# A decoder step on one core: half of the quarter-stack requests of tiles 3 to 6 asked for by ScalarE

## The chip, the cores and the metric

The kernel runs on one core of a Trainium2 chip. Its time is the device time of one execution in microseconds. The profile is of one execution, taken by the hardware profiler. PE is TensorE's matmul stream, DVE is VectorE, ACT is ScalarE, POOL is GpSimd, SP is SyncE. "SPq" and "ACTq" mark requests for transfers (DMAs) that an engine issues; the transfers themselves run on the core's 16 DMA engines.

## The reference

One layer of a decoder over 1024 prompt tokens and 32 sample tokens, in float32. A combined projection feeds latent attention and a chunked retention; both are gated, mixed, added to the input and normalised (`h`). Then comes the part around the change: a shared expert, and for each token 6 of 64 routed experts, summed with weights, and a last normalisation:

```
eidx, ew = route(h2d, w_router, router_bias)              # 6 experts and weights for a token
ffn = routed_experts(h2d, eidx, ew, ...) + swiglu(h2d, w_sh_gate, w_sh_up, w_sh_down)
y   = layer_norm(DEEPNORM_ALPHA * h + ffn, ln2_g, ln2_b)
```

`routed_experts` multiplies each token's row by the gate, up and down matrices of its six experts and adds the six results, each times its weight.

## The kernel before, in words

Tokens lie in nine tiles of 128 rows (`NT = 9`, `P = 128`, `D = 1024`); tile 8 holds only the 32 sample tokens. The kernel runs in stages one after the other: projection, retention, attention, mixing, trunk (normalisation and routing), experts. The change is at the end of `experts`.

In the expert stage a loop goes over blocks of up to 128 gathered token rows, one expert each. TensorE multiplies, and GpSimd scatters each block's results to the table `y_rows` in HBM (`put_rows`, L2470). That table has 8 rows of 4 KB for each token, of which rows 0 to 5 are its six experts' results. Each scatter increments `y_out[c]`.

The last stage adds the six rows of each token with their weights, adds the shared expert's result and alpha times `h`, and normalises. For tiles 0 to 7 the work is split:

- rows 4 and 5 of each token come as a "pair" (1 MB a tile, `pair`, L2379) and are added to `acc[t]` by VectorE (`add_row`, L2656), two additions a tile in the order of the tiles; each increments `added`.
- rows 0 to 3 come as a "stack" of 2 MB a tile (`stack`, L2386): four quarters q of 512 KB, each with the 32 tokens 32q to 32q+31 of the tile, 128 rows of 4 KB. Each quarter is one transfer and adds 16 to `stack_in[b]`. TensorE sums them with 16 small matmuls against a weight matrix (`routed`, L2890) after `stack_in[b]` has reached 64 times the use of that buffer.
- the shared expert's down product of a tile is eight matmuls (`shared_down`, L2863) into the same accumulator before `routed`. TensorE issues it two tiles ahead: after those of tiles 0, 1, 3 and 2 the order is routed 0, routed 1, routed 2, shared 4, routed 3, shared 5, and so on. There are four accumulators `S` (e_G, e_T, e_Y, e_A); the shared product of tile i waits until tile i-4 is joined.
- the sample tokens (tile 8) have their own small rows (`small`, L2390), a small shared product (L2867) and a small routed product (L2876).

VectorE then works tile by tile: `join` (L2716, alpha times `acc` plus the accumulator, with the row sum), `mean`, `scaled` of the tile before (L2755), `variance`, `gain` (L2745). ScalarE computes the sums of squares (`squares`, L2563), GpSimd the reciprocal root (L2493). SyncE writes each finished tile out (L2447).

Seven stack buffers serve eight tiles (`stack_of`). Tiles 0, 1 and 2 use buffers that expert weights held; tiles 3, 4, 5 and 6 use memory in which the pairs of tiles 0 to 7 lay, so their requests wait until those pairs are added; tile 7 uses the buffer of tile 0 again and waits for `pe_done`, which `routed` increments.

All of these requests are issued by SyncE, in this order: after the last rows are written (`rows_written(NE)`, a wait for both `y_out`) the stacks of tiles 0, 1, 2; then for tiles 3 to 6 a wait `pair_added(2 * t - 5)`, which is `added >= 4, 8, 12, 16`, and the stack; then a wait for `pe_done` and the stack of tile 7; then the six small rows; then the outputs as they become ready. ScalarE issues none in this stage. An engine carries its instructions out in order, and SyncE and ScalarE have a hardware queue each in front of the same 16 DMA engines (queue 1 and queue 10 in the profile).

Of the kernel before, what the change touches and what calls it, by code (L numbers as in the profile page):

```python
# [28 lines left out]
P = 128  # L29
D = 1024  # L30
KD = D // P
NT = 9
# [17 lines left out]
NE, TOPK, FF = 64, 6, 256  # L50
# [10 lines left out]
NS = DB * DQ  # L61
# [2191 lines left out]
def experts(nc, passed, begun, parts, acc_in, acc, pair_in, pairs, stack_in, stacks, w_stack, sel, small_rows, junk, shared, ident, wb, gu_in, ready, w_d, d_in, ln2, ln2_rows, ln2_in, a, h_rows, tok_list, meta, y_rows, out_p, out_s):  # L2253

    with ExitStack() as ctx:
        sb = lambda n, s, d=F32: ctx.enter_context(nc.sbuf_tensor("e_" + n, s, d))
        sem = lambda n: ctx.enter_context(nc.semaphore("e_" + n))
        W = 4
# [14 lines left out]
        stacks = stacks + [nc.alloc_sbuf_tensor_at("stack6", [P, 4, D], F32, offset=w_hi_at)]  # L2273
# [14 lines left out]
        small_w_ok, small_ok, pl, diag_ok, part_ok, pe_done, added, joined, shift_ok, sq_ok, var_ok, rstd_ok, gained, out_ok, o_out = [  # L2288
            sem(n) for n in "small_w_ok small_ok pl diag_ok part_ok pe_done added joined shift_ok sq_ok var_ok rstd_ok gained out_ok o_out".split()]
        stack_of = [(5, 1), (3, 1), (6, 1), (0, 1), (4, 1), (1, 1), (2, 1), (5, 2)]  # L2290
# [5 lines left out]
        y_out = [sem(f"y_out{c}") for c in range(2)]  # L2296
# [6 lines left out]
        def wait_alone(eng, s, value):  # L2303
            eng.wait_ge(s, value)
            eng.sem_inc(passed, 1)

        def quads(eng):

            return eng.value_load(meta[P:P + 1, 0:1], min_val=1, max_val=OVER // W)
# [4 lines left out]
        def at(eng, r, mul, add):  # L2314

            return r * mul + add if isinstance(r, int) else eng.snap(r * mul + add)
# [7 lines left out]
        def _(sp):  # L2324
# [8 lines left out]
            more = quads(sp)  # L2333
# [45 lines left out]
                sp.dma_start(pairs[t][:].rearrange("p k n -> p (k n)"),  # L2379
                             y_rows.rearrange("(t k) n -> t (k n)", k=8)[t * P:(t + 1) * P, 4 * D:6 * D]).then_inc(pair_in[t], 16)  # L2380

            def stack(t):

                b = stack_of[t][0]
                for q in range(4):
                    sp.dma_start(stacks[b][:, q, :], y_rows.rearrange("(t k) n -> t k n", k=8)[t * P + NS * q:t * P + NS * (q + 1), 0:4, :]).then_inc(stack_in[b], 16)  # L2386

            def small(k):
# [16 lines left out]
            def pair_added(t):  # L2405

                sp.wait_ge(added, 2 * t + 2)
# [27 lines left out]
            for t in range(3):  # L2435
                stack(t)
            for t in range(3, NT - 2):
                pair_added(2 * t - 5)
                stack(t)
            sp.wait_ge(pe_done, 1)  # L2440
            stack(NT - 2)
            for k in range(TOPK):
                small(k)
# [51 lines left out]
        @block.scalar  # L2495
        def _(act):
            s_ = nc.scalar

            def gate(n, c):
                act.wait_ge(gu_done, n)  # L2500
                s_.activation(sig[:, c, :], G[c][:, 0:FF], ACT.Sigmoid).then_inc(sig_ok, 1)

            def turned_act(n, c):
                act.wait_ge(a_turned, n)
                s_.copy(aT[:, c].rearrange("p k n -> p (k n)"), A[:, 0:2 * P]).then_inc(aT_ok, 1)

            def turned(n, c):
                act.wait_ge(x_turned, n)
                s_.copy(xT_hi[:, c].rearrange("p k n -> p (k n)"), GX[1][:].rearrange("p q n -> p (q n)")).then_inc(xT_act, 1)  # L2509

            def rounded(s, n_in, c, part):
                act.wait_ge(gu_in[s], n_in)
                for j in (2 * part, 2 * part + 1):
                    s_.copy(w_hi[c][:, :, 2 * j:2 * j + 2, :], w_gu[s][:, :, 2 * j:2 * j + 2, :]).then_inc(w_hi_ok, 1)  # L2514

            def kept(n, c, stored):
                act.wait_ge(d_done, n)
                if stored is not None:
                    wait_alone(act, y_out[c], stored)
                s_.copy(y_sb[:, c, 0:512], Y[0][:]).then_inc(y_act, 1)  # L2520

            gate(1, 0)
            for s in range(1, W):
                turned(2 * s + 4, 1 - s % 2)
                for part in range(2):
                    if s >= 2:
                        if part == 0:
                            kept(s - 1, s % 2, None)
                        rounded((s + 1) % W, 16 if s < W - 1 else 32, 1 - s % 2, part)
                    if part == 0:  # L2530
                        turned_act(s, 1 - s % 2)
                gate(s + 1, s % 2)
            more = quads(act)

            def four(r, last=False):
                for s in range(W):
                    c, n_in = s % 2, at(act, r, 16, 16 if s < W - 1 else 32)
                    if not (last and s == W - 1):
                        turned(at(act, r, 2 * W, 2 * s + 4), 1 - c)
                    kept(at(act, r, W, s - 1), c, at(act, r, 8 * W, 16 * (s // 2) - 16))  # L2540
                    if not (last and s == W - 1):
                        rounded((s + 1) % W, n_in, 1 - c, 0)
                    turned_act(at(act, r, W, s), 1 - c)
                    if not (last and s == W - 1):
                        rounded((s + 1) % W, n_in, 1 - c, 1)
                    gate(at(act, r, W, s + 1), c)
            with act.Fori(1, more + (NE // W - 1)) as r:
                four(r)
            four(act.snap(more + (NE // W - 1)), last=True)
            r = act.snap(more + NE // W)  # L2550
            kept(at(act, r, W, -1), 0, at(act, r, 8 * W, -16))
            turned_act(at(act, r, W, 0), 1)
            kept(at(act, r, W, 0), 1, at(act, r, 8 * W, -16))
            for j in range(4):
                act.wait_ge(spread_ok, j + 1)
                s_.copy(ln2[:, j // 2, 512 * (j % 2):512 * (j % 2 + 1)], AS[:, j % 2, :]).then_inc(ln2_ok, 1)

            def squares(i):
                t = LAST_ORDER[i]
                act.wait_ge(shift_ok, i + 1)  # L2560
                act.wait_ge(sq_ok, i)
                if t < NT - 1:
                    s_.activation(junk[:, 2], acc[t][:], ACT.Square, bias=shift[:, t:t + 1], accum_out=sums[:, t, 1:2]).then_inc(sq_ok, 1)  # L2563
                else:
                    s_.activation(junk[:, 2, 0:QW], last_acc, ACT.Square, bias=shift[:, t:t + 1], accum_out=sums[:, t, 1:2]).then_inc(sq_ok, 1)
            for i in range(NT):
                squares(i)
                if i == 1:
                    act.wait_ge(ln2_ok, 4)
                    for q in range(4):  # L2570
                        own = slice(NS * q, NS * (q + 1))
                        s_.copy(last_g[own], g2[own, QW * q:QW * (q + 1)]).then_inc(ln2_small_ok, 1)
                        s_.copy(last_b[own], b2[own, QW * q:QW * (q + 1)]).then_inc(ln2_small_ok, 1)
# [552 lines left out]
```

## Time and profile before

| what | value |
|---|---|
| times of three runs | 1779.93, 1784.15, 1787.57 us |
| median | 1784.15 us |
| profiled execution, its own time | 1784.89 us |
| its span, first to last instruction | 1782.8 us |
| mean granted clock of TensorE | 0.990 |
| PE busy | 1716.1 us (96%) |
| DVE busy | 1056.9 us (59%) |
| ACT busy | 682.5 us (38%) |
| POOL busy | 333.8 us (19%) |
| queue 1 (SyncE's): packets, MB | 120052, 337.69 |
| queue 10 (ScalarE's): packets, MB | 2880, 17.04 |

The span is measured from the first to the last instruction; the execution's own time has some 2 us around it. Busy shares are means over all stages, which have different limits; the last stage, from 1712 us on, is 71 us of the 1782.8. Times in rows are from the span's start.

### The profile page before, as it was taken

The page shows a single profiled execution, that of the slowest core. Times are in us where ns is not written, and L with a number is a line of the kernel's source. Part 1 is how long each engine was busy: PE and PEld are TensorE (multiplying, and loading weights), DVE is VectorE, ACT ScalarE, POOL GpSimd, SP SyncE. Part 2 cuts the span into 40 slices and gives each one's busy share as a digit, 9 for nine tenths or more (in the row PEclk, how much of TensorE's full clock was granted, in tenths as well). Part 3 has the DMA queues.
Part 4 walks back from the last instruction along what each step waited for, and adds up shares of the span by engine and source line. Part 5 has one row for each costly group of instructions (what it writes and reads, how often), then busy time and mean ns, then how long its engine had stood idle before and what let it go on. Part 6 is the DMA issues. An engine that isn't in the chain of part 4 may idle for free. (4 is left out here: it accounts for less than half of the span.)

```text
span 1782.8 us, 27306 instructions
## 1 busy us (share of the span) xinstructions
PE 1716.1 (96%) x9548; PEld 1325.8 (74%) x9548; DVE 1056.9 (59%) x1729; ACT 682.5 (38%) x1104; POOL 333.8 (19%) x283
## 2 busy tenths in 40 slices
PE   9999999999999999999998889999999999999986
PEld 9999999999956555997874556767677676767742
DVE  3112443534436554755587747777777777787776
ACT  3112212213145544302110145656556565666512
POOL 0000321403010000000126442212222222222112
PEclk9999999999999999999999999999999999999998
DMA  6332534334123132624333489999999999999899
GB/s 222 91 89 91 149 104 148 114 125 155 62 89 86 42 87 97 248 102 156 93 146 122 134 301 360 398 384 405 391 405 386 391 401 386 399 382 378 341 360 341
DMA packets 144355, 408.35 MB, mean 229 GB/s; under 512 B 29916, under 2 KB 92036, under 8 KB 125700
## 3 DMA queue, kind: packets, MB, share of 16 engines
q1 hardware_dynamic: 120052, 337.69, 51.7%
q0 software_dynamic: 21344, 52.59, 7.7%
q10 hardware_dynamic: 2880, 17.04, 2.4%
q8 instruction: 47, 0.77, 0.2%
q14 instruction: 32, 0.26, 0.1%
HBM read 359.08 MB, written 67.80 MB: 239 GB/s over the span
## 5 line engine op out<-in xcount | busy, mean ns | idle before, releaser
L2799 PE MATMUL e_Y<-mixT,e_aT 128*128 128x512 f32 x544 | 246.2, 595 | 8.0 <-issue 7.0
L2810 PE MATMUL e_G<-w_lo,xT_hi 128*128 128x512 f32 x528 | 205.7, 390 | 0.0
L2799 PEld LDWEIGHTS e_Y<-mixT,e_aT 128*128 128x128 f32 x544 | 103.1, 190 | 113.1 <-issue 108.2
L2606 DVE TENSOR_TENSOR w_lo<-wb,e_w_hi 128x1024 fp32r<-128x1024 f32 x132 | 155.2, 1219 | 19.6 <-ACT e_w_hi L2514 19.5
L2606 DVE TENSOR_TENSOR w_lo<-wb,half_hi 128x1024 fp32r<-128x1024 f32 x128 | 150.5, 1219 | 11.1 <-ACT half_hi L2514 10.4
L2599 DVE TENSOR_TENSOR xT_lo<-e_T,xT_hi 128x1024 fp32r<-128x1024 f32 x66 | 80.8, 1224 | 126.6 <-ACT xT_hi L2509 124.6
L1323 PE MATMUL banks<-x_hi,gw_hi 128*128 128x352 f32 x464 | 151.6, 327 | 1.4 <-DVE r_srg L1115 1.4
L1323 PE MATMUL banks<-x_hi,gw_lo 128*128 128x352 f32 x464 | 149.2, 322 | 0.0
L1323 PE MATMUL banks<-x_lo,gw_hi 128*128 128x352 f32 x464 | 148.9, 321 | 0.0
L2509 ACT CAST xT_hi<-e_T 128x1024 fp32r<-128x1024 f32 x66 | 67.1, 1017 | 204.2 <-PE e_T L2788 200.3
L187 PE MATMUL banks<-w_hi,x_hi 128*128 128x244 f32 x512 | 142.0, 277 | 1.3 <-DVE x_lo L244 1.3
L187 PE MATMUL banks<-w_hi,x_lo 128*128 128x244 f32 x512 | 141.2, 276 | 0.0
L187 PE MATMUL banks<-w_lo,x_hi 128*128 128x244 f32 x512 | 140.9, 275 | 0.0
L2514 ACT CAST e_w_hi<-wb 128x1024 fp32r<-128x1024 f32 x132 | 132.0, 1052 | 6.2 <-DMA wb<-in_w_exp_gu 6.1
L2514 ACT CAST half_hi<-wb 128x1024 fp32r<-128x1024 f32 x128 | 127.9, 1051 | 7.4 <-DMA wb<-in_w_exp_gu 7.4
L2464 POOL DMA_INDIRECT xg<-d_h_rows,g_idx x64 | 66.1, 1032 | 307.9 <-PE e_T L2788 284.0
L2470 POOL DMA_INDIRECT d_y_rows<-pages,e_s_idx x68 | 82.2, 1209 | 219.0 <-DVE pages L2611 202.1
L2810 PEld LDWEIGHTS e_G<-w_lo,xT_hi 128*128 128x128 f32 x528 | 99.7, 189 | 16.8
L2810 PE MATMUL e_G<-e_w_hi,xT_hi 128*128 128x512 f32 x264 | 109.1, 413 | 0.2 <-DVE w_lo L2606 0.2
L2810 PE MATMUL e_G<-half_hi,xT_hi 128*128 128x512 f32 x264 | 109.1, 413 | 0.0
L2810 PE MATMUL e_G<-e_w_hi,xT_lo 128*128 128x512 f32 x264 | 103.7, 393 | 0.0
L2810 PE MATMUL e_G<-half_hi,xT_lo 128*128 128x512 f32 x264 | 103.7, 393 | 0.0
(472 smaller groups left out, 3560.3 us busy)
## 6 DMA issues: line engine op xcount, KB each, us to landing
wb<-in_w_exp_gu SPq DMA_DIRECT2D x64, 2048.0 KB
mixT<-in_w_exp_dn SPq DMA_DIRECT2D x68, 1024.0 KB
stack<-d_y_rows SPq DMA_DIRECT2D x32, 512.0 KB, 14.7
gw_sb<-in_w_gate SPq DMA_DIRECT2D x20, 512.0 KB, 6.7
d_proj<-o_sb SPq DMA_DIRECT2D x8, 1098.0 KB, 5.9
d_gateT<-r_g_out ACTq DMA_DIRECT2D x16, 528.0 KB, 2.6
pages<-in_cache_both SPq DMA_DIRECT2D x64, 128.0 KB, 2.0
wb<-in_w_exp_gu ACTq DMA_DIRECT2D x4, 2048.0 KB
```

Of the source, the lines that this page charges most:

```text
L187: mm = nc.tensor.matmul(ps[:, j % 4, 0:CW], x[:, k, rows(t)], w[:, c, k, :], start=k == 0 and i == 0, stop=k == KD - 1 and i == 2)
L1323: mm = t_.matmul(ps[6 + u % 2][:, 0:TC], w[:, n % 2, k, :], x[:, k, c * TC:(c + 1) * TC], start=k == 0 and s == 0, stop=k == KD - 1 and s ...
L2464: g.indirect_dma_start(xg[s][:], None, h_rows, bass.IndirectOffsetOnAxis(ap=g_idx[s][:, 0:1], axis=0), bounds_check=XT - 1, oob_is_err=Fal ...
L2470: g.indirect_dma_start(y_rows, bass.IndirectOffsetOnAxis(ap=s_idx[s][:, 0:1], axis=0), y_sb[:, c, :], None, bounds_check=8 * XT - 1, oob_i ...
L2509: s_.copy(xT_hi[:, c].rearrange("p k n -> p (k n)"), GX[1][:].rearrange("p q n -> p (q n)")).then_inc(xT_act, 1)
L2514: s_.copy(w_hi[c][:, :, 2 * j:2 * j + 2, :], w_gu[s][:, :, 2 * j:2 * j + 2, :]).then_inc(w_hi_ok, 1)
L2599: v.tensor_tensor(xT_lo[:, c].rearrange("p k n -> p (k n)"), GX[1][:].rearrange("p q n -> p (q n)"), xT_hi[:, c].rearrange("p k n -> p (k ...
L2606: v.tensor_tensor(w_lo[s][:, :, at_k, :], w_gu[s][:, :, at_k, :], w_hi[c][:, :, at_k, :].bitcast(F32), ALU.subtract).then_inc(w_lo_ok, 1)
L2799: mm = t_.matmul(Y[q][:], aT[:, c, k, :], w_d[:, s, k, q * 512:(q + 1) * 512], start=k == 0, stop=k == 1)
L2810: mm = t_.matmul(G[c], x[:, c, k, :], w[:, :, k, :], start=k == 0 and i == 0, stop=k == KD - 1 and i == 2)
```

## The change

SyncE asks for quarters 0 and 1 only of the stacks of tiles 3, 4, 5 and 6. Quarters 2 and 3 of these tiles are asked for by ScalarE, into the same buffers and with the same semaphores. ScalarE does so after its four copies of the last normalisation's parameters (L2556) and before its first `squares`; it waits for both `y_out` counters and then, for each tile, for the same count of `added` as SyncE does. Tiles 0, 1, 2 and 7 stay whole with SyncE.

```diff
-            def stack(t):
+            def stack(t, parts=range(4)):
                 b = stack_of[t][0]
-                for q in range(4):
+                for q in parts:
                     sp.dma_start(stacks[b][:, q, :], y_rows.rearrange("(t k) n -> t k n", k=8)[t * P + NS * q:t * P + NS * (q + 1), 0:4, :]).then_inc(stack_in[b], 16)
...
             for t in range(3, NT - 2):
                 pair_added(2 * t - 5)
-                stack(t)
+                stack(t, range(2))
             sp.wait_ge(pe_done, 1)
             stack(NT - 2)
...
+            def stack_half(t):
+                b = stack_of[t][0]
+                for q in range(2, 4):
+                    act.dma_start(stacks[b][:, q, :], y_rows.rearrange("(t k) n -> t k n", k=8)[t * P + NS * q:t * P + NS * (q + 1), 0:4, :]).then_inc(stack_in[b], 16)
             for j in range(4):
                 act.wait_ge(spread_ok, j + 1)
                 s_.copy(ln2[:, j // 2, 512 * (j % 2):512 * (j % 2 + 1)], AS[:, j % 2, :]).then_inc(ln2_ok, 1)
...
+            for c in range(2):
+                wait_alone(act, y_out[c], act.snap(more * (8 * W) + 8 * NE))
+            for t in range(3, NT - 2):
+                act.wait_ge(added, 2 * (2 * t - 5) + 2)
+                stack_half(t)
             for i in range(NT):
                 squares(i)
```

## Rows read from the trace of the kernel before

**Rows 1.** The page's 40 equal slices: DMA share in tenths, rate.
```profile
DMA  6332534334123132624333489999999999999899
GB/s 222 91 89 91 149 104 148 114 125 155 62 89 86 42 87 97 248 102 156 93 146 122 134 301 360 398 384 405 391 405 386 391 401 386 399 382 378 341 360 341
```

**Rows 2.** The chain of waits, last stage: start us, duration us, what.
```profile
1749.53 18.36 DMA stack<-d_y_rows
1768.02 3.25 PE e_A L2890 x16
1771.30 1.24 DVE acc L2716 x2
...
1778.85 0.48 DVE acc L2757
```

**Rows 3.** Stretches: length, busy us of each engine, PEclk, DMA share, GB/s.
```profile
1720.00:1722.00 2.00, 2.00 (x6) 0.95 (x5) 2.00 (x2) 0.00 (x0) 0.00 (x0) 1.00 0.51 115
1722.00:1724.00 2.00, 2.00 (x6) 0.85 (x5) 1.33 (x2) 0.00 (x0) 0.00 (x0) 1.00 1.07 414
1724.00:1763.00 39.00, 33.54 (x159) 11.07 (x161) 22.33 (x35) 10.17 (x20) 9.04 (x6) 0.96 1.02 405
1763.00:1768.00 5.00, 0.88 (x19) 0.27 (x9) 3.94 (x6) 1.24 (x2) 1.51 (x1) 0.93 1.02 254
...
1732.00:1737.40 5.40, 3.33 (x16) 0.69 (x16) 1.70 (x3) 1.21 (x2) 1.47 (x1) 0.68 1.03 416
```

**Rows 4.** TensorE in order of time, 1728 to 1772: start, duration, instructions, [idle before].
```profile
1728.53 1.92 PE L2890 MATMUL e_G<-stack,w_stack 128*32 128x512 f32 x16 [0.17 <-DMA stack<-d_y_rows]
1733.64 3.33 PE L2890 MATMUL e_T<-stack,w_stack 128*32 128x512 f32 x16 [3.19 <-DMA stack<-d_y_rows]
1738.76 1.92 PE L2890 MATMUL e_Y<-stack,w_stack 128*32 128x512 f32 x16 [1.79 <-DMA stack<-d_y_rows]
1740.62 3.70 PE L2863 MATMUL e_G<-pages 128*128 128x512 f32 x8
...
1762.83 1.05 PE L2867 MATMUL e_G<-pages 128*32 128x256 f32 x16
1768.02 3.21 PE L2890 MATMUL e_A<-stack,w_stack 128*32 128x512 f32 x16 [4.14 <-DMA stack<-d_y_rows]
```

**Rows 5.** The stack requests, L2386: all; then the first five's issue times and landing.
```profile
1719.24 31.36 SPq L2386 DMA_DIRECT2D stack<-d_y_rows  x32
...
L2386 SPq DMA_DIRECT2D stack<-d_y_rows x5: 580/603/661, 1719.2 to 1721.9; - x5
DMA to landing us min/median/max: 4.2/6.4/7.8
```

**Rows 6.** VectorE in order of time: pair additions, then join and gain of tiles 6, 7.
```profile
1711.05 1.27 DVE L2656 SCALAR_TENSOR_TENSOR acc<-pair,e_w_part,acc 128x1024 f32<-128x1024 f32 x1
1713.21 10.16 DVE L2656 SCALAR_TENSOR_TENSOR acc<-pair,e_w_part,acc 128x1024 f32<-128x1024 f32 x8 [0.89 <-DMA acc<-d_h_rows]
...
1763.08 1.22 DVE L2716 SCALAR_TENSOR_TENSOR acc<-acc,e_Y 128x1024 f32<-128x1024 f32 x1 [1.41 <-PE e_Y L2890]
...
1765.88 1.27 DVE L2745 SCALAR_TENSOR_TENSOR acc<-acc,e_shift 128x1024 f32<-128x1024 f32 x1
1771.30 1.22 DVE L2716 SCALAR_TENSOR_TENSOR acc<-acc,e_A 128x1024 f32<-128x1024 f32 x1 [4.14 <-PE e_A L2890]
```

**Rows 7.** ScalarE in order of time: its last parameter copy and first squares.
```profile
1717.90 0.59 ACT L2556 COPY acc<-e_A 128x512 f32<-128x512 f32 x1 [0.28 <-PE e_A L2898]
1731.97 1.15 ACT L2563 ACTIVATE junk<-early,e_shift 128x1024 f32<-128x1024 f32 x1 [13.48 <-DVE e_shift L2729]
```

**Rows 8.** DMA packets of 936 to 948 us: all; then by queue (packets, MB, share).
```profile
DMA packets 671, 4.79 MB, mean 399 GB/s; under 512 B 211, under 2 KB 211, under 8 KB 435
...
q10 hardware_dynamic: 265, 3.87, 79.8%
q1 hardware_dynamic: 256, 0.92, 20.4%
```

## The prediction, made before the changed kernel ran

> **What bounds the kernel now.** I read the page's forty slices first. The DMA rates there stand near 400 GB/s from the middle of the expert stage on and through the last stage [rows 1]. Then I read the chain of waits from the end backwards. It closes with the four steps of [rows 2]: a stack transfer asked for at 1749.53 us that needs 18.36 us, the routed matmuls of tile 7, the join on VectorE, and the last VectorE pass at 1778.85. So the end is set by the last stack piece, and what follows it is a fixed tail: from the join of tile 7 (1771.30) to the end of the span (1782.8) are 11.5 us.
>
> The next view is the one by stretches [rows 3]. The DMA engines start late after the last expert rows are written (115 GB/s between 1720 and 1722), then they are full: share 1.02 at 405 GB/s for 39 us. The reader should see that this is 39 us x 405 GB/s = 15.8 MB, almost all of the 32 quarter stacks of 512 KB (16.8 MB). SyncE's issuing isn't the limit: in the first microseconds a request takes it about 0.6 us [rows 5], and 524 KB in 0.6 us would be 870 GB/s. The later requests are stretched only because the DMA queue is full: they land 15 us after their issue. From 1763 to 1768 the share stays 1.02 and the rate falls to 254 GB/s; the last quarter lands in that dip.
>
> TensorE's own rows [rows 4] show two regimes. Tiles 0, 1 and 2 wait for their stacks: the routed matmuls start at 1728.53, 1733.64 and 1738.76, 5.1 us apart, which is one stack of 2.10 MB at 409 GB/s. From tile 2 on TensorE doesn't wait. It alternates a routed product (1.9 us) and the shared expert's product of the tile two ahead (3.7 us), about 5.5 us a tile, and so falls behind the arriving stacks. It comes to rest at 1762.83 + 1.05 = 1763.88 and waits 4.14 us for tile 7's stack. That 4.14 us is all the room between TensorE's row of work and the transfer that now sets the end.
>
> **The change, part by part.**
> *Requests moved.* Eight of SyncE's 32 quarter requests go to ScalarE: quarters 2 and 3 of tiles 3, 4, 5 and 6. On SyncE they are hidden already by the full queue; taking eight out saves nothing, since the other 24, the six small ones and the outputs still follow at the rate at which data drains. Value 0.
>
> *ScalarE's new work.* It waits for both y_out counters (rows written, 1719.2 by SyncE's first request [rows 5]), then for `added`. Its last copy ends at 1717.90 + 0.59 = 1718.5 and the next instruction behind the new ones, the squares of tile 0, starts at 1731.97 [rows 7]. The counts that it waits for are 4, 8, 12 and 16; 8 are there at 1711.05 + 1.27 = 1712.3, and eight more follow from 1713.21 in 10.16 us, so 12 is there at 1718.3 and 16 at 1723.4 [rows 6]. Six requests of 0.6 us end at about 1722.9, the last two at 1724.6. Squares of tile 0 have 7 us of cover and they move later anyway, see below. Cost 0; if a request took as much as SyncE's do behind a full queue (1.1 to 1.6 us), eight would still end by 1732.
>
> *What the second queue does to the order.* This is the part with a price. Before, all quarters stood in one queue in the order in which TensorE wants them. Now ScalarE's eight quarters, 4 MB (binary, as below), are asked for at once from 1719.2 on, beside SyncE's quarters of tiles 0, 1 and 2. Nothing ties them to their turn: their buffers are free early, which is just what the added counts above say. The total of bytes is the same and the engines are full, so each early megabyte for tiles 3 to 6 is a megabyte later for tiles 0 to 2. How two hardware queues share is seen in one stretch: at 936 to 948 us queue 10 carried 16 KB packets of the first expert weights (asked for by ScalarE) while queue 1 carried SyncE's 4 KB rows; 265 packets against 256, at 399 GB/s together [rows 8]. That is one packet each in turn. In the last stage all packets are 4 KB, so I take equal shares.
>
> The Trainium skill, "DMA: Bandwidth & Descriptors", section "Queues, rings and completion order", says that each DMA engine goes round-robin over the queues it has work for, a packet at a time. The counts in [rows 8] agree; with the reverse, SyncE's queue served first, the sum below would be 0.
>
> One MB at 409 GB/s takes 2.56 us. Before, 2, 4 and 6 MB had landed when tiles 0, 1 and 2 started. Now both queues deliver 1:1 until ScalarE's 4 MB are through, that is until 8 MB in total. Tile 0 (2 MB of SyncE's) is there after 4 MB: 1733.6. Tile 1 after 8 MB: 1733.64 + 4 x 2.56 = 1743.9. Tile 2 after 10 MB: 1738.76 + 4 x 2.56 = 1749.0, which is 10.25 us later than before. Tiles 3, 4, 5 and 6 then need only 1 MB each and land at 1751.6, 1754.1, 1756.7 and 1759.2, all before TensorE wants them (1754.5 and every 5.5 us). Tile 7 lands as before, at most 1767.9. It waits for `pe_done` of tile 0, about 1736, while SyncE comes to it only when eight of its 20 earlier quarters have landed, about 1744: no wait.
>
> *What TensorE and VectorE do with it.* TensorE's row from the routed product of tile 2 to the end of the small product takes 1763.88 - 1738.76 = 25.1 us with no wait in it [rows 4]. Started at 1749.0 it ends at 1774.1, and tile 7's stack has then long landed: the 4.14 us wait is gone. Tile 7's product follows at once, in 1.9 us at the full clock (it took 3.25 before, at the clock granted after its wait), and ends at 1776.0. Late next is VectorE. Tile 6 is joined at 1763.08 + 10.25 = 1773.3 and its gain pass ends 4.07 us later (1765.88 + 1.27 against 1763.08 [rows 6]), at 1777.4. Only then is tile 7's join executed; before it began at 1771.30. So the tail of 11.5 us starts 6.1 us later. That is 10.25 - 4.14.
>
> *Sum.* 0 + 0 + 10.25 - 4.14 = +6.1 us. The span goes from 1782.8 to 1788.9, the profiled execution from 1784.89 to 1791.0. That execution lies 0.7 us above the median of the three runs (1784.15), the runs reach from 1779.93 to 1787.57; I say 1790.5.
>
> *Bounds of what the trace doesn't show.* (a) Sharing of two queues with equal packets: at one end SyncE's queue goes first, 0 us; at the other all of ScalarE's 4 MB lie ahead of tile 2, which is my value; more than 4 MB can't. I take the value beside [rows 8]. (b) Throughput of two interleaved queues: the mixed stretch gave 399 GB/s against 409, so 8 MB would take 0.5 us more; the far end is the dip's 254 GB/s, 33 instead of 20.5 us, +12.5. I take 0, near the mixed row. Below zero lies the slow start: 1720 to 1722 has room of 1.4 us, which a second issuer might fill. (c) TensorE's clock when tile 2 starts: the stretch 1732 to 1737.4 has a granted clock of 0.68, after TensorE had idled from 1730.5, and tile 1's product there took 3.33 us for 1.92. Tile 2 started at the full clock, 1.8 us of idling behind tile 1. In the new order the spacing from tile 1 to tile 2 is the same 5.1 us, so I take full clock, 0; the other end is one or two such half-speed stretches laid on tile 2's row, +1.7 to +3.4 us (half of the 3.4 us that 0.68 over 5.4 us amounts to).
>
> **The rivals.**
> *Half clock at tile 2 (slower).* TensorE idles from 1728.4 to 1733.6, from about 1737 to 1743.9 and from 1747 to 1749, more than before. If its clock is at the 1.2 GHz level when tile 2 starts and for 6.8 us more, the row of 25.1 us, which has no slack any more, grows by 3.4. It decides from a loss of 2.8 us on: +9.5 us, 1794, slower by 0.53%. For it: [rows 3], 0.68 after an idle of 3 us. Against: tile 2's own start before, at full speed in the same spacing.
> *Interleaving slows the engines (slower).* If the alternating reads run like the dip, tile 2 is late by another 12.5: 1803. Against it is the 399 GB/s.
> *The order holds (no change).* If SyncE's queue is served first, or ScalarE's requests come through late, tiles 0 to 2 are on time, TensorE rests at 1763.9 again and the last bytes land at 1767.9 as the bytes are the same: 1784. The "change that does nothing" is the same case. Against: 265 packets to 256.
> *More throughput (faster).* If two queues fill the start and shorten the dip in which tile 7's last quarter sits, up to 4.1 us go: 1780. It needs tile 2 on time as well. Against: share 1.02 over 39 us, nothing left to fill. The same skill page, section "Issuing engines are not separate DMA queues", says that transfers started by several engines run on the same 16 DMA engines and that only the sequencer's time for starting them is saved; the page's rule gives this rival nothing, and the full share agrees.
>
> **How the numbers follow.** Forecast (+4 to +8 us): 0.62. Half clock: 0.14. Slow interleaving, in part or in full: 0.08. Order holds: 0.12. More throughput: 0.04. What this kernel's measurement can tell from no change is about 0.5%, 8.9 us. Slower than that are the slow interleaving, most of the clock case and the upper edge of the forecast together with the runs' own spread of 4 us either way: 0.25. Faster than that would need twice the 4.1 us: 0.03. Within: 0.72. The range takes in the case without change at its low end and the clock case at its high end: 1783 to 1798; the likeliest case alone has 1788 to 1793.
>
> **What would show it.** Right: stack packets on both queue 1 and queue 10 after 1721, in equal numbers until about 1742; routed products of tiles 0, 1, 2 at 1733.6, 1743.9 and 1749.0; TensorE without a wait from there to the end of tile 7's product; VectorE's join of tile 7 directly behind the gain pass of tile 6; ScalarE's requests over by 1725. Wrong: tile 0 starting at 1728.5 would end the sharing argument; a wait of TensorE for tile 3's stack or later would mean that the halves come otherwise than in turn; a stage rate off 405 GB/s would end the sum of bytes; half clock in 1749 to 1756 puts the clock rival in its place.

## The result: slower by about half a percent, and where it shows in the profile after

| | before | changed |
|---|---|---|
| median of the first six runs each | 1786.54 us | 1795.91 us |
| ratio, 95% interval | | 1.0056 [1.0032, 1.0080] |
| the same, measured anew with 11 runs (before: 28) | 1780.6 us | 1787.34 us, 1.0044 [1.0024, 1.0064] |
| profiled execution, span | 1782.8 us | 1792.3 us |
| last stage: from SyncE's first stack request to the end of the span | 63.6 us | 68.0 us |

The forecast was +6.1 us, 1790.5 us in a range of 1783 to 1798, with the largest chance on "within 0.5%". The median of 1795.91 us lies in the range, but above the 1788 to 1793 named for the likeliest case. The medians lie 9.4 us apart in the first measurement and 6.7 us in the second; the first ratio is just beyond 0.5% and the second just inside. Neither interval reaches 1.

The two spans differ by 9.5 us, but only 4.4 us of that arise in the last stage. The other 5.1 us are there before a changed instruction is reached: the first stack request stands at 1724.32 in place of 1719.24 [rows 5]. The repeats below show that this start moves by several microseconds with no change to the program, so all times of the stage are told from its own first request ("+28.5" is 28.5 us after it).

SyncE's and ScalarE's requests in order of time (start, duration, what, count):

```profile
1724.32 29.41 SPq L2386 DMA_DIRECT2D stack<-d_y_rows  x24
1753.77 5.13 SPq L2390 DMA_DIRECT2D small_rows<-d_y_rows  x6
...
1724.33 6.06 ACTq L2558 DMA_DIRECT2D stack<-d_y_rows  x8
1742.88 1.15 ACT L2568 ACTIVATE junk<-early,e_shift 128x1024 f32<-128x1024 f32 x1 [19.21 <-DVE e_shift L2739]
```

ScalarE is through with its eight requests in 6.1 us, 12.5 us before its squares of tile 0. The packets of the 19 us in which both queues are full, 1727 to 1746:

```profile
DMA packets 2137, 7.83 MB, mean 412 GB/s; under 512 B 225, under 2 KB 225, under 8 KB 2137
...
q1 hardware_dynamic: 1074, 3.94, 51.5%
q10 hardware_dynamic: 1063, 3.89, 50.9%
```

They take turns, 1074 to 1063, and together move 412 GB/s. The two queues share the rate of one. The Trainium skill, "DMA: Bandwidth & Descriptors", section "Queues, rings and completion order", has the round by packets between queues; these rows agree with it (a packet of that page may hold several of those counted here, and equal counts don't tell which of the two is the unit). Stretches of the profile after, which answer to [rows 3]:

```profile
1724.30:1726.00 1.70, 1.70 (x5) 0.76 (x4) 1.67 (x2) 0.00 (x0) 0.00 (x0) 1.00 0.32 34
1726.00:1728.00 2.00, 2.00 (x6) 0.95 (x5) 1.96 (x3) 0.00 (x0) 0.00 (x0) 1.00 0.83 289
1728.00:1767.00 39.00, 26.86 (x112) 8.34 (x111) 16.55 (x26) 7.68 (x16) 6.01 (x4) 0.87 1.03 411
1767.00:1771.50 4.50, 4.50 (x23) 1.48 (x22) 2.95 (x7) 1.24 (x2) 1.51 (x1) 1.00 1.03 247
```

The share is full and the rate even, as before; the slow stretch at the end of the stacks is there too. Now TensorE in order of time, the answer to [rows 4]:

```profile
1737.83 3.54 PE L2900 MATMUL e_G<-stack,w_stack 128*32 128x512 f32 x16 [4.29 <-DMA stack<-d_y_rows]
1747.74 3.64 PE L2900 MATMUL e_T<-stack,w_stack 128*32 128x512 f32 x16 [6.38 <-DMA stack<-d_y_rows]
1752.85 1.92 PE L2900 MATMUL e_Y<-stack,w_stack 128*32 128x512 f32 x16 [1.47 <-DMA stack<-d_y_rows]
...
1776.54 1.05 PE L2877 MATMUL e_G<-pages 128*32 128x256 f32 x16
1777.40 1.90 PE L2900 MATMUL e_A<-stack,w_stack 128*32 128x512 f32 x16
```

Tiles 0, 1 and 2 start at +13.5, +23.4 and +28.5; before it was +9.3, +14.4 and +19.5. From tile 2 on there is no wait any more, not for tile 7's stack either. VectorE at the end, the answer to [rows 6]:

```profile
1779.58 1.28 DVE L2755 SCALAR_TENSOR_TENSOR acc<-acc,e_shift 128x1024 f32<-128x1024 f32 x1
1780.78 1.21 DVE L2726 SCALAR_TENSOR_TENSOR acc<-acc,e_A 128x1024 f32<-128x1024 f32 x1
```

The join of tile 7 (second row) follows the gain pass of tile 6 with no idle time; in [rows 6] VectorE had waited 4.14 us for TensorE there. From this join to the end of the span are 11.5 us, the same tail as before (1780.78 to 1792.3). The chain of waits has changed in the same way: the transfer that ended before tile 2's product is in it, and from there on TensorE's own work:

```profile
1732.18 20.54 DMA stack<-d_y_rows
1752.72 0.14 issue
1752.85 1.92 PE e_Y L2900 x16
1754.78 3.63 PE e_G L2873 x8
...
1774.86 1.90 PE e_Y L2900 x16
```

### The profile page after: what moved, and what is told of

Read it like the earlier page. It is cut to its first block and busy times, and to the rows that moved or that the text cites. A ratio compares the mean times of both kernels' runs of the same rounds, so it can differ in the third digit from the quotient of the medians.

```text
span 1792.3 us, 27309 instructions
## 1 busy us (share of the span) xinstructions
PE 1717.3 (96%) x9548; PEld 1324.5 (74%) x9548; DVE 1056.9 (59%) x1729; ACT 681.5 (38%) x1104; POOL 333.9 (19%) x283
## 5 line engine op out<-in xcount | busy, mean ns | idle before, releaser
L2616 DVE TENSOR_TENSOR w_lo<-wb,e_w_hi 128x1024 fp32r<-128x1024 f32 x132 | 154.6, 1220 | 23.7 <-ACT e_w_hi L2514 23.6
```

The source lines that it names most:

```text
L2616: v.tensor_tensor(w_lo[s][:, :, at_k, :], w_gu[s][:, :, at_k, :], w_hi[c][:, :, at_k, :].bitcast(F32), ALU.subtract).then_inc(w_lo_ok, 1)
```

## The experiments

Theory O: the loss comes from the order in which the bytes arrive; what is asked for early for tiles 3 to 6 is late for tiles 0 to 2. Rival Q: the second queue costs something by itself. Rival U: the changed program also loses time ahead of the stage. Each ratio is to the kernel before, measured beside the run.

**The kernel before, again.** No edit.

> The kernel before once more, unchanged, for the spread of the part ahead of the last stage. Measured as stage length: from SyncE's first stack request to the end of the span, 63.6 us in the first profile (1719.2 to 1782.8). Theory O (the loss is in the last stage and comes from the order in which the bytes arrive): stage again 63 to 64 us, ratio 1.000 within 0.003; the start of the stage may vary by some us from run to run. Rival U (the changed kernel also lost some 5 us ahead of the stage, because its program is another): the stage starts again at 1719 within 1 us in this kernel.

Ratio 1.0016 [0.9997, 1.0035]. The first request is at 1719.01, the span 1780.1, the stage 61.1 us. The start within 1 us of 1719 is what rival U expected of this run; the next run decides on it. The stage is 2.5 us shorter than in the first profile of the same kernel. Two differences account for it. Tile 7's last quarter was there for a product at +47.6 and not +48.8, and that product ran at the full clock (1.92 us against 3.21 in [rows 4]):

```profile
1738.07 3.50 PE L2890 MATMUL e_Y<-stack,w_stack 128*32 128x512 f32 x16 [3.20 <-DMA stack<-d_y_rows]
...
1766.58 1.92 PE L2890 MATMUL e_A<-stack,w_stack 128*32 128x512 f32 x16 [2.13 <-DMA stack<-d_y_rows]
```
```profile
1768.56 1.22 DVE L2716 SCALAR_TENSOR_TENSOR acc<-acc,e_A 128x1024 f32<-128x1024 f32 x1 [0.84 <-PE e_A L2890]
```

So my 63 to 64 us was too narrow: the stage of the kernel before is 61.1 to 63.6 us. It also shows tile 2's product at half speed, which cost nothing here, because 2.1 us of waiting for tile 7 were left after it. The last row is VectorE's join of tile 7. It waited 0.84 us here and 4.14 us in [rows 6], and this wait is the slack that counts: a delay of TensorE's row reaches the end of the span once VectorE has none left.

**The changed kernel, again.** No edit.

> The changed kernel once more, unchanged. Theory O: stage length again 68.0 us (67.5 to 68.5), its start anywhere between 1717 and 1726 like in the kernel before, ratio 1.0025 plus the spread, so 1.000 to 1.006. Rival U: stage start again at 1724 within 1 us, 5 us later than before, ratio 1.005 to 1.006.

Ratio 1.0044 [1.0024, 1.0064]. The first request is at 1714.94, 4.3 us earlier than in the kernel before and 9.4 us earlier than in the first profile of this same program. That is also earlier than the 1717 to 1726 that I had given. Rival U is out: the later start of the first profile doesn't come back with the same program. For programs that are the kernel before up to this request (`sp_order`, `small_late`, `small_early` below) it varies in the same way, 1718.29 to 1724.80. What moves it is open. The stage is 70.0 us, beyond my 67.5 to 68.5. The tiles arrive as in the first profile (+13.7, +23.4, +28.6), but the clock was at its lower level when tile 2 began. Three rows of TensorE, and then the stretch of the first (PEclk is the third number from the end):

```profile
1743.50 3.64 PE L2900 MATMUL e_Y<-stack,w_stack 128*32 128x512 f32 x16 [1.48 <-DMA stack<-d_y_rows]
1747.07 3.93 PE L2873 MATMUL e_G<-pages 128*128 128x512 f32 x8
1750.93 1.93 PE L2900 MATMUL e_A<-stack,w_stack 128*32 128x512 f32 x16
```
```profile
1743.50:1747.10 3.60, 3.60 (x17) 0.68 (x17) 2.56 (x3) 3.49 (x9) 1.51 (x1) 0.50 1.04 412
```

From tile 2's start to tile 3's are 7.43 us in place of 5.49, and the 1.94 us more are all in the end: the row of TensorE has no wait left in which they could vanish.

**One queue, the order of two.** SyncE alone; the eight early quarters stand between the first eight of tiles 0 and 1. (`stack` takes `parts` as in the changed kernel.)

```diff
...
-            for t in range(3):
-                stack(t)
-            for t in range(3, NT - 2):
-                pair_added(2 * t - 5)
-                stack(t)
+            early_half = [(t, q) for t in range(3, NT - 2) for q in range(2, 4)]
+            for i, (t, q) in enumerate([(t, q) for t in range(3) for q in range(4)]):
+                stack(t, [q])
+                if i < 8:
+                    if i % 2 == 0:
+                        pair_added(2 * early_half[i][0] - 5)
+                    stack(early_half[i][0], [early_half[i][1]])
+            for t in range(3, NT - 2):
+                stack(t, range(2))
```

> SyncE alone, one queue, but asking in the order that one-to-one sharing gave: quarter of tile 0, quarter 2 of tile 3, quarter of tile 0, quarter 3 of tile 3, and so on; the eight late quarters stand between the first eight of tiles 0 and 1. Theory O (order): tiles 0, 1 and 2 start late as with two queues, routed product of tile 2 28.5 to 30 us after the first request (19.5 before), stage length 68 to 69.5 us, 1 us more than the changed kernel if the second issuer shortened the slow start. Rival Q (the second queue itself costs: contention between queues, ScalarE's requests): stage length 63.6 us as before.

Ratio 1.0080 [1.0054, 1.0105]; first request 1721.93, span 1793.1, stage 71.2 us.

```profile
1735.35 3.59 PE L2894 MATMUL e_G<-stack,w_stack 128*32 128x512 f32 x16 [3.98 <-DMA stack<-d_y_rows]
1745.59 3.64 PE L2894 MATMUL e_T<-stack,w_stack 128*32 128x512 f32 x16 [6.65 <-DMA stack<-d_y_rows]
1752.00 3.18 PE L2894 MATMUL e_Y<-stack,w_stack 128*32 128x512 f32 x16 [2.77 <-DMA stack<-d_y_rows]
1755.11 4.10 PE L2867 MATMUL e_G<-pages 128*128 128x512 f32 x8
```

Tiles 0, 1 and 2 at +13.4, +23.7 and +30.1: without any second queue the delay is all there and more. Tiles 0 and 1 are complete here after 3.5 and 7.5 MB and not after 4 and 8, because their last quarter stands ahead of the early one beside it; tile 2 needs 10 MB in both kernels and came 1.5 us later than with two queues. Rival Q is out, and theory O stands. The stage is 1.7 us above my upper figure, 1.65 of it from the half clock at tile 2 (7.14 us from tile 2 to tile 3, for 5.49).

**Two queues, the order of one.** From the changed kernel, ScalarE takes its half of tiles 0, 1 and 2 too.

```diff
             for t in range(3):
-                stack(t)
+                stack(t, range(2))
...
+            for t in range(3):
+                stack_half(t)
             for t in range(3, NT - 2):
                 act.wait_ge(added, 2 * (2 * t - 5) + 2)
                 stack_half(t)
```

> Two queues for all tiles 0 to 6: quarters 0 and 1 by SyncE, 2 and 3 by ScalarE, each in the order of the tiles; tile 7 by SyncE. Theory O: routed products of tiles 0, 1, 2 start 8 to 9.3, 13 to 14.4 and 18.3 to 19.5 us after the first request, the stage takes 62.3 to 63.6 us; the lower ends if two issuers fill the slow start (1.2 us). Rival Q (the second queue costs by itself): tiles 0 to 2 late and the stage at 67 us or more. ScalarE has 14 requests; if its queue fills at about 12 it is held until about 1731, squares of tile 0 at most 2 us late, hidden.

Ratio 0.9998 [0.9979, 1.0016]; first request 1711.59, span 1772.2, stage 60.6 us.

```profile
1711.59 25.19 SPq L2386 DMA_DIRECT2D stack<-d_y_rows  x18
...
1711.60 14.04 ACTq L2558 DMA_DIRECT2D stack<-d_y_rows  x14
```
```profile
1724.92 2.92 PE L2902 MATMUL e_T<-stack,w_stack 128*32 128x512 f32 x16 [2.17 <-DMA stack<-d_y_rows]
1730.04 3.64 PE L2902 MATMUL e_Y<-stack,w_stack 128*32 128x512 f32 x16 [2.20 <-DMA stack<-d_y_rows]
...
1758.91 1.92 PE L2902 MATMUL e_A<-stack,w_stack 128*32 128x512 f32 x16 [1.29 <-DMA stack<-d_y_rows]
```

Tiles 1 and 2 at +13.3 and +18.5, 0.6 to 1.1 us earlier than with one queue. The stretches from +4 to +9, before and here, show where it comes from:

```profile
1723.24:1728.24 5.00, 5.00 (x12) 1.90 (x11) 0.13 (x1) 0.00 (x0) 0.00 (x0) 1.00 1.02 370
1715.59:1720.59 5.00, 5.00 (x13) 2.09 (x11) 0.41 (x1) 0.00 (x0) 0.00 (x0) 1.00 1.02 418
```

All ten profiles agree: in this stretch the five with one issuer ran at 365 to 376 GB/s, the five with two at 418 to 421, both with a share of 0.98 to 1.03. From +9 to +17 all ran at 410 to 417. So a full DMA share was not the full rate. In the first 4 us two issuers brought no clear gain. Why one issuer is slower from +4 to +9 is open. ScalarE was held by its requests until +14.1 (one of them took 5.2 us), which set back its squares of tile 0 and, as far as the rows show, nothing on the path. Tile 2's product ran at half clock here too (3.64 us), tile 3's came 8.34 us after it and not 5.49, and VectorE's join of tile 7 had no wait left. The stage is under my 62.3 to 63.6. It is 0.5 us under the best profile of before, less than two profiles of one kernel differ by, and a ratio can't show it.

**Half the dose.** ScalarE takes its half of tiles 3 and 4 only; SyncE has tiles 5 and 6 whole.

```diff
-                stack(t, range(2))
+                stack(t, range(2) if t < 5 else range(4))
...
-            for t in range(3, NT - 2):
+            for t in range(3, 5):
                 act.wait_ge(added, 2 * (2 * t - 5) + 2)
```

> Half the dose: ScalarE asks for quarters 2 and 3 of tiles 3 and 4 only (2 MB ahead of their turn in place of 4); the rest as in the changed kernel. All times from SyncE's first stack request. Theory O (order, and 4.1 us of slack in TensorE's row): tile 2's product starts 5.1 us later than before, at 23.2 to 24.6 (19.1 to 19.5 before, 28.5 changed); of these 5.1 us the slack covers all but 1 to 3, so the stage takes 63 to 65.5 us (61.1 and 63.6 before, 67.9 and 70.0 changed) and most of the loss is gone. Rival L (no slack, each microsecond of tile 2 costs one): 66 to 68 us.

Ratio 1.0003 [0.9983, 1.0023]; first request 1717.81, span 1780.7, stage 62.9 us.

```profile
1741.21 1.92 PE L2900 MATMUL e_Y<-stack,w_stack 128*32 128x512 f32 x16 [1.48 <-DMA stack<-d_y_rows]
...
1765.76 1.90 PE L2900 MATMUL e_A<-stack,w_stack 128*32 128x512 f32 x16
```
```profile
1769.14 1.21 DVE L2726 SCALAR_TENSOR_TENSOR acc<-acc,e_A 128x1024 f32<-128x1024 f32 x1
```

Tile 2 at +23.4, 3.9 to 4.3 us later than in the two profiles of before, tile 7 at +47.95, where those had +47.6 and +48.8. VectorE's join of tile 7 has no wait any more (last row). So the first 4 us of delay used up the slack: the stage is 0.7 us shorter than in the first profile of before and 1.8 us longer than in the second. The next 5.1 us (to the changed kernel's +28.5) cost 5.1 us: 62.9 to 68.0. The stage is just under my 63 to 65.5, and rival L, which wanted 66 to 68, is out. The size of the slack is less sure than that it exists: 4.14 us of waiting on VectorE in one profile of before, 0.84 us in the other.

**The sample tokens' rows later, earlier, and with both queues.** The stretch of 254 GB/s in [rows 3] begins where the six small requests stand in the queue. They are moved: behind the output of tile 0 (`small_late`, and with both queues in order `both_small_late`), or between the stacks of tiles 2 and 3 (`small_early`).

```diff
-            for k in range(TOPK):
-                small(k)
             for i, t in enumerate(LAST_ORDER):
                 sp.wait_ge(out_ok, i + 1)
                 if t < NT - 1:
                     sp.dma_start(out_p[t * P:(t + 1) * P, :], acc[t][:]).then_inc(o_out, 16)
+                    if i == 0:
+                        for k in range(TOPK):
+                            small(k)
```

> One queue as before, but the six requests for the sample tokens' rows stand behind the output of tile 0 and no longer straight behind tile 7's stack. Theory D (the stretch of 250 GB/s at the end of the stacks is the slow reading of those rows, and tile 7's last quarter is caught in it): the last quarter lands about 44.5 us after the first request, tile 7's product starts when TensorE's row is through, 44.6 to 46.5 (47.6 and 48.8 before), stage 59.5 to 61.5 us. Rival E (the stretch belongs to the end of the stacks or to the output writes that begin there): the rate falls at 44 us again, product of tile 7 at 47.5 or later, stage 61 to 64 us.

Ratio 1.0004 [0.9982, 1.0026]; first request 1718.29, stage 60.6 us.

The edit of `small_early`:

```diff
             for t in range(3):
                 stack(t)
+            for k in range(TOPK):
+                small(k)
             for t in range(3, NT - 2):
...
             stack(NT - 2)
-            for k in range(TOPK):
-                small(k)
```

> One queue as before, the six requests for the sample tokens' rows between the stacks of tiles 2 and 3. Theory D: the stretch of about 250 GB/s moves to some 19 to 24 us after the first request, tile 3's product is held to about 28 us, tile 7's last quarter lands in an even stream at 47 to 48 us, so the stage stays at 61 to 63.6 us. Rival E: no slow stretch at 19 to 24 us beyond 2 us, and it stays at the end of the stacks.

Ratio 1.0016 [0.9994, 1.0037]; first request 1724.80, stage 63.5 us. Two stretches of it, +17.2 to +23.2 and +38.2 to +48.2:

```profile
1742.00:1748.00 6.00, 2.13 (x16) 0.68 (x16) 3.94 (x6) 3.96 (x10) 1.51 (x1) 0.78 1.04 272
1763.00:1773.00 10.00, 10.00 (x58) 3.50 (x60) 6.91 (x12) 2.48 (x4) 3.03 (x2) 1.00 1.03 411
```

The slow stretch has gone where the small rows went: 272 GB/s there, an even 411 at the end of the stacks. Theory D holds in this. Tile 2's product came at +21.2, 1.7 to 2.2 us late, although its stack stands ahead of the small rows in the queue: the quarter before them is caught in the stretch, as tile 7's was. Two expectations failed. Tile 3's product came at +29.5, after a wait of 1.19 us, and not at about +28; tile 7's came at +49.9, and its last quarter was to land at +47 to +48. Why it came so late in an even stream is open.

With the rows late (`small_late`), tile 7's product started at +47.1, not at +44.6 to 46.5 as expected, and TensorE then also waited for the small rows:

```profile
1765.43 1.92 PE L2891 MATMUL e_A<-stack,w_stack 128*32 128x512 f32 x16 [1.48 <-DMA stack<-d_y_rows]
1768.23 1.21 PE L2877 MATMUL e_G<-small_rows,e_diag_small 128*32 128x256 f32 x16 [0.88 <-DMA small_rows<-d_y_rows]
```

The slow stretch began near +45 here and near +43 before, so it moved with the rows again, by about the 1.3 us that an output of 512 KB takes. But one output between the two doesn't free the last quarter. Why it doesn't is open.

The third kernel has both edits, two queues in the order of one and the small rows late.

> Both queues for all of tiles 0 to 6 in the order of the tiles, and the sample tokens' rows behind the output of tile 0. Theory D with the quicker start of two issuers: last quarter about 43.5 us after the first request, tile 7's product at 44 to 46, stage 58.5 to 60.5 us (60.7 with both queues alone), ratio to the kernel before 0.998 to 0.9995. Rival E: 60.7 us as without the move.

Ratio 0.9988 [0.9968, 1.0009], the lowest ratio of all, and not told apart from 1. First request 1722.27, stage 60.9 us. The stage is above my 58.5 to 60.5, next to the 60.7 that rival E gave. The moved rows weren't what failed: tile 7's product came without a wait, at +46.0. But TensorE's tile 2 ran at half clock (8.38 us to tile 3, for 5.49), VectorE had no wait left before the join of tile 7, and so the gain was spent. The small rows came 1.27 us late as well.

## Why the prediction came out

*The rate bounds the stage, a second queue adds nothing to it.* Right for the stage as a whole: 411 GB/s over 39 us with share 1.03, 405 and 1.02 before. Wrong for its beginning: from +4 to +9 two issuers moved 419 GB/s where one had moved 370. The prediction had put one issuer's requests at 870 GB/s, so no limit, and had read the share of 1.02 as "nothing left to fill". The share hid a rate a tenth lower.

*The queues share packet by packet.* Right: 1074 to 1063.

*Tile 2 comes 10.25 us late.* The mechanism was right, the size 1.2 us too large: 28.5 - 19.5 = 9.0. Tiles 0, 1 and 2 all came 0.9 to 1.3 us before the forecast's +14.4, +24.7 and +29.8. The term that I had named as a bound, up to 1.4 us from a second issuer, and valued at 0, was there, though not in the microseconds from 1720 to 1722 where I had looked for it. Over the first 10 us one issuer moved 296 to 308 GB/s on average and two moved 326 to 331, which is worth 0.4 to 0.9 us. The rest of the 1.2 us isn't explained. With one queue in the same order tile 2 came at +30.1, 1.5 us later than with two.

*TensorE's row takes up 4.14 us of it.* The mechanism was right, the size holds for one profile. TensorE's row goes through without a wait in 24.7 us (25.1 before, where tile 4 had still waited 0.3 us for its stack, which I had overlooked). The slack that reaches the end is VectorE's wait before the join of tile 7. In the first profile it was 4.14 us, by chance the same as TensorE's; 1.3 us of it came from the last product at half clock. In the second it was 0.84 us, where TensorE had waited 2.13. Half the dose shows the slack from the other side: 4 us of delay used it up, and from there on it was one for one.

*VectorE is late next, the tail is 11.5 us.* Right, both in the rows above: the join straight behind the gain pass, and 11.5 us to the end.

*The sum, +6.1 us.* In the stage: 9.0 - 4.14 - 0.4 = 4.5, measured 4.4 for the first pair of profiles; the second pair gives 70.0 - 61.1 = 8.9. The two pairs differ by the clock at tile 2, which costs the changed kernel 1.9 us and the kernel before nothing, and by the 2.5 us between the two profiles of before (tile 7's stack 1.2 us earlier, its product 1.3 us shorter). The mean of the pairs is 6.6 us, 0.37%, which lies in both intervals. That 6.1 lies so near it is partly luck: the delay was 1.2 us too large, the slack was taken from the profile that had more of it, and the clock was put at 0. Of the 5.4 us between the forecast of 1790.5 and the median, 2.4 are the kernel before's own median, 1786.54 over six runs and not 1784.15.

*Half clock at tile 2* (a rival at 0.14) is no rival but a part: it happened in one of two profiles of the changed kernel, and in one of two of the kernel before. In all ten profiles tile 2's product took 3.18 to 3.64 us in seven and 1.92 us in three. I had argued from the one profile, where it ran at full speed, that the same spacing gives the same clock. It doesn't. I should have put at least half of its 1.9 us into the sum.

*ScalarE's cost 0.* Right: through at +6.1, next needed at +18.6.

*More throughput, interleaving slow, order holds.* None decided the result; of the first, the faster microseconds from +4 to +9 are a small part. The 5 us ahead of the stage in the first pair of profiles are not the change's: the first stack request stood at 1711.6 to 1724.8 in ten profiles, and 9.4 us apart for one and the same program.

## What to carry to other kernels

When the DMA engines are full, a transfer that may start early takes its bytes from the one that is needed first: a second queue undoes an order that a single one keeps. Split each tile over both queues in the order of use, or leave it on one. To price a delay, first find how long the work behind it can still wait and what follows when that is gone. Read this at the last engine of the chain, and in more than one profile: here it was 4.1 us in one and 0.8 us in another, and the half clock at tile 2, which had cost the kernel before nothing, cost 1.9 us once the wait was gone. A full DMA share is not proof of the full rate; read the GB/s beside it. And read a stage from its own first event where the stages ahead of it scatter more than the change is worth.

## What the runs showed of the hardware

- Two hardware queues with 4 KB packets share in turns, 1074 to 1063, at the rate of one (412 GB/s).
- From 4 to 9 us after the first request one issuer moved 365 to 376 GB/s and two moved 418 to 421, at the same full DMA share; before and after there was no such difference. The Trainium skill, "DMA: Bandwidth & Descriptors", section "Issuing engines are not separate DMA queues", grants a second issuer only the sequencer's time for starting transfers; whether this gain is that time, no run shows, and none shows a gain beyond it.
- ScalarE was held while it issued 14 requests of 512 KB (14 us, the longest of them 5.2 us) and not with 8 (6 us, the longest 0.9 us).
- The stretches in which the sample tokens' table rows were read (32 KB apart) ran at 247 to 272 GB/s with the DMA share full, both at the end of the stacks and when they were moved ahead of tile 3's. Moved there, they delayed tile 2's product, whose transfer stands right ahead of them, by 1.7 to 2.2 us. That the spacing of the rows is the reason is an inference, not tried.
- TensorE's granted clock at the start of tile 2 was at either of its levels (2.4 and 1.2 GHz) in the two profiles of the changed kernel, though both had tile 1's product at the lower level, 5.1 us between the starts of tiles 1 and 2, and 1.47 and 1.48 us of idling before it.
